# RWKV heads: nine wide elementwise products per head pair move from VectorE to GpSimd, and three preparation steps change places

## The reference

```python
r, k, v, wl, al, gl = jnp.split(pm, [...], axis=-1)
w = -jax.nn.softplus(-(decay_w0 + jnp.tanh(wl) @ decay_w2)) - 0.5      # decay, as a log rate
a = jax.nn.sigmoid(iclr_a0 + al @ iclr_a2)                             # rate
g = jax.nn.sigmoid(gl) @ gate_g2                                       # gate
kk = k * k_k
kk = kk / jnp.maximum(jnp.sqrt(jnp.sum(kk * kk, axis=-1)), 1e-12)      # unit keys
k = k * (1.0 + (a - 1.0) * k_a)                                        # k_mod
decay = jnp.exp(-jnp.exp(w))
def step(S, inp):
    sa = jnp.einsum('bhvk,bhk->bhv', S, kk_t)
    S = S * d_t - sa[..., None] * (kk_t * a_t) + v_t[..., None] * k_t
    return S, jnp.einsum('bhvk,bhk->bhv', S, r_t)
S, y = lax.scan(step, s0, ...)
yn = (y - mean(y)) * rsqrt(var(y) + GN_EPS) * lnx_w + lnx_b            # per head
bonus = sum(r * k * r_k) * v
return (yn + bonus) * g
```

## Time and profile before

| | us |
|---|---|
| median of 3 runs | 3746.51 |
| lowest and highest | 3738.27, 3763.45 |
| the profiled execution's own time | 3749.47 |
| its span, first to last instruction | 3747.8 |
| PE busy | 3337.5 (89%) |
| DVE busy | 3037.3 (81%) |
| ACT busy | 1127.8 (30%) |
| POOL busy | 1597.2 (43%) |
| mean granted TensorE clock | 0.936 of full speed |

### The profile page before, as it was taken

How to read it: one execution, slowest core, us unless ns; L and a number is a source line. 1 busy time by engine, 2 the same in 40 slices (tenths; PEclk the granted TensorE clock), 3 DMA queues, 4 the chain that set the end, 5 groups by cost and what they waited for, 6 DMA issues and landing times.

```text
span 3747.8 us, 62513 instructions
## 1 busy us (share of the span) xinstructions
PE 3337.5 (89%) x21071; PEld 3085.6 (82%) x21071; DVE 3037.3 (81%) x6175; ACT 1127.8 (30%) x2153; POOL 1597.2 (43%) x1407
## 2 busy tenths in 40 slices
PE   7998848888887998847779999999999999999997
PEld 7998736666676755547779999999999999999997
DVE  6543656676664689989789999999999999999997
ACT  3101433233231222369722222222222222222221
POOL 1120001111110133520067776767777676676772
PEclk9999778787898999979989999999999999999998
DMA  3222330010004001024699999999999999999995
GB/s 122 97 87 78 111 103 7 22 33 13 1 10 160 13 26 37 15 93 190 247 348 362 356 352 339 353 348 366 353 348 359 350 355 349 334 363 347 350 356 188
DMA packets 296942, 781.44 MB, mean 209 GB/s; under 512 B 28376, under 2 KB 129240, under 8 KB 295424
## 3 DMA queue, kind: packets, MB, share of 16 engines
q0 software_dynamic: 135568, 493.54, 35.9%
q1 hardware_dynamic: 161264, 286.56, 21.4%
HBM read 709.32 MB, written 70.11 MB: 208 GB/s over the span
## 4 chain that ended last, share of the span: by engine, by line
PE 30%; DVE 9%; issue 7%; DMA 6%; POOL 2%; DVEq 1%; ACT 1%; POOLq 0%; ACTq 0%; SPq 0%
PE experts_down_ps L113 7%; PE experts_down_ps L114 7%; PE experts_down_ps L115 7%; DMA stream_u<-in_up_rows,experts_u_at 4%; PE experts_up_ps L114 3%; PE experts_up_ps L113 3%; PE experts_up_ps L115 3%; DVE stream_u L3315 2%; DVE stream_h_rows_of L3332 2%; DMA stream_u<-in_down,experts_v_at 2%; POOL stream_u L3102 1%; DVE stream_h L3338 1%; DVE picking_mean_square L2880 1%; DVE stream_h_rest L2880 1%; POOL stream_u L3087 1%
## 5 line engine op out<-in xcount | busy, mean ns | idle before, releaser
L3087 POOL DMA_INDIRECT stream_u<-in_up_rows,experts_u_at x448 | 600.2, 1340 | 316.6 <-DVE experts_dot L3315 150.1
L3102 POOL DMA_INDIRECT stream_u<-in_down,experts_v_at x448 | 588.6, 1314 | 253.3 <-issue 95.7
L113 PE MATMUL experts_up_ps<-experts_u_hi,experts_up_hi 128*128 128x320 f32 x2048 | 634.8, 310 | 33.5 <-DVE experts_up_lo L3286 27.2
L113 PE MATMUL experts_down_ps<-experts_act_hi,experts_down_hi 128*128 128x320 f32 x2048 | 640.6, 313 | 21.0 <-DVE stream_h L3338 15.7
L114 PE MATMUL experts_down_ps<-experts_act_lo,experts_down_hi 128*128 128x320 f32 x2048 | 636.1, 311 | 0.0
L115 PE MATMUL experts_down_ps<-experts_act_hi,experts_down_lo 128*128 128x320 f32 x2048 | 636.1, 311 | 0.0
L114 PE MATMUL experts_up_ps<-experts_u_lo,experts_up_hi 128*128 128x320 f32 x2048 | 634.1, 310 | 0.0
L115 PE MATMUL experts_up_ps<-experts_u_hi,experts_up_lo 128*128 128x320 f32 x2048 | 634.0, 310 | 0.0
L3332 DVE SCALAR_TENSOR_TENSOR stream_h_rows_of<-stream_u,experts_weight,stream_h_rows_of 128x1024 f32<-128x1024 f32 x448 | 568.1, 1280 | 30.4 <-DMA stream_u<-in_down,experts_v_at 19.0
L3315 DVE CUSTOM_DVE_ANT_0 stream_u<-stream_u,stream_u_rows_of 128x1024 f32<-128x1024 f32 x448 | 544.7, 1216 | 40.3 <-DMA stream_u<-in_up_rows,experts_u_at 40.2
L113 PEld LDWEIGHTS experts_up_ps<-experts_u_hi,experts_up_hi 128*128 128x128 f32 x2048 | 385.7, 188 | 34.7 <-DVE experts_up_lo L3286 34.2
(11 more groups left out here) (463 smaller groups left out, 6143.7 us busy)
## 6 DMA issues: line engine op xcount, KB each, us to landing
stream_h_rest<-in_up SPq DMA_DIRECT2D x128, 512.0 KB, 7.1
stream_u<-in_down_pieces SPq DMA_DIRECT2D x128, 512.0 KB, 6.3
gates<-spread_spread SPq DMA_DIRECT2D x10, 4096.0 KB, 11.5
experts_gates<-gates SPq DMA_DIRECT2D x64, 640.0 KB, 9.9
cols<-inp_done POOLq DMA_DIRECT2D x26, 576.0 KB, 3.8
inp_w_in<-in_w_in SPq DMA_DIRECT2D x27, 512.0 KB, 4.4
pick_w_query<-in_w_query SPq DMA_DIRECT2D x14, 512.0 KB, 4.0
stream_u<-in_up_rows,experts_u_at POOLq DMA_INDIRECT x448, 7.1
```

The costliest lines, as they stand in the source:

```text
L113: pe.matmul(out, w_hi, x_hi, start=start, stop=False)
L3087: pool.indirect_dma_start((half_row if i == HALF_DOT else u_row[b]), None, up_rows_d, bass.IndirectOffsetOnAxis(ap=u_at[slot][:, col:col + ...
L3102: pool.indirect_dma_start((half_row if i == HALF_ADD else v_row[b]), None, v_table, bass.IndirectOffsetOnAxis(ap=v_at[slot][:, col:col + 1 ...
```

## The change

For pairs 1 to 3, five products of the preparation (`in_log`, `before_log`, `k_mod`, `kk`, `b`) are issued on GpSimd, in two functions: `logs` in g2 of the pair before, and `unit_keys` in g3, each ahead of that group's `list_blocks`. For pairs 0 to 2, the four products of the epilogue go to GpSimd as `normed_y`, in g1 after the stores of the sample states. New semaphores `prep_pool` and `ep_pool` count them. The first pair's preparation and the last pair's epilogue stay on VectorE. Besides, `norm` moves from steps 9 to 11 to steps 6 to 8 and `gate` from 6 to 8 to 9 to 11; the exponentials move from steps 6 to 9 to steps 9 to 12, the clipping from 12 to 9, the reciprocals of the norm from 13 to 15 to 10 to 12, and `weighted` from 17 to 16.

```diff
@@ -1003,12 +1003,13 @@
-PREP_PE = ("decay0", "decay1", "decay2", "rate0", "rate1", "rate2", "gate0", "gate1", "gate2", "norm0", "norm1", "norm2",
+PREP_PE = ("decay0", "decay1", "decay2", "rate0", "rate1", "rate2", "norm0", "norm1", "norm2", "gate0", "gate1", "gate2",
            "bonus0", "bonus1", "bonus2")
-PREP_ACT = ("decay0", "decay1", "square", "decay2", "rate0", "rate1", "rate2", "gate0", "exp_inv", "gate1", "exp_in", "gate2",
-            "exp_before", "exp_next", "exp_seq", "norm0", "norm1", "norm2")
-PREP_DVE = ("kk_raw", "less_ka", "log_rate", "cum", "mid", "in_log", "before_log", "next_diff", "next_log", "k_scale", "k_mod",
-            "clipped", "inverse0", "inverse1", "inverse2", "kk", "b", "weighted", "bonus0", "bonus1", "bonus2")
+PREP_ACT = ("decay0", "decay1", "square", "decay2", "rate0", "rate1", "rate2", "norm0", "norm1", "norm2", "gate0", "exp_inv", "gate1", "exp_in", "gate2",
+            "exp_before", "exp_next", "exp_seq")
+PREP_DVE = ("kk_raw", "less_ka", "log_rate", "cum", "mid", "next_diff", "next_log", "k_scale",
+            "clipped", "inverse0", "inverse1", "inverse2", "weighted", "bonus0", "bonus1", "bonus2")
+PREP_POOL = ("in_log", "before_log", "k_mod", "kk", "b")
...
-DECAY_AT, RATE_AT, GATE_AT, NORM_AT, INVERSE_AT, BONUS_AT = 0, 3, 6, 9, 13, 19
+DECAY_AT, RATE_AT, NORM_AT, GATE_AT, EXP_AT, INVERSE_AT = 0, 3, 6, 9, 9, 10
...
-EP_VEC = ("mean0", "mean1", "var0", "var1", "mean2", "var2", "inverse0", "inverse1", "inverse2", "scaled", "affine", "with_bonus", "gated")
+EP_VEC = ("mean0", "mean1", "var0", "var1", "mean2", "var2", "inverse0", "inverse1", "inverse2")
+EP_POOL = ("scaled", "affine", "with_bonus", "gated")
...
+def on_pool(j, name):
+    return j > 0 and name in PREP_POOL
...
+        def wait_prepared(eng, j, name):
+            if on_pool(j, name):
+                eng.wait_ge(prep_pool, reached(PREP_POOL, j, name))
+            else:
+                eng.wait_ge(prep_vec, reached(PREP_DVE, j, name))
+
+        def mid_log_args(pre):
+            by_tile = [buf[:].rearrange("p (c t) -> p c t", c=NT) for buf in (pre.in_decay, cum)]
+            return *by_tile, mid[:, 0:NT].unsqueeze(2).broadcast_to([P, NT, P])
...
+                def made(j, name):
+                    pool.wait_ge(ep_pool, reached(EP_POOL, j, name))
+
+                def normed_y(j):
+                    y, pre = y_of[j % 2], prepared[j % 2]
+                    pool.wait_ge(ep_vec, reached(EP_VEC, j, "inverse2"))
+                    pool.tensor_tensor(y[:], y[:], pre.inv_decay[:], ALU.mult).then_inc(ep_pool, 1)
+                    made(j, "scaled")
+                    pool.tensor_scalar(y[:], y[:], coef(j, C_LNW), coef(j, C_LNB), ALU.mult, ALU.add).then_inc(ep_pool, 1)
+                    made(j, "affine")
+                    pool.wait_ge(prep_vec, reached(PREP_DVE, j, "bonus2"))
+                    pool.tensor_tensor(y[:], y[:], pre.bonus[:], ALU.add).then_inc(ep_pool, 1)
+                    made(j, "with_bonus")
+                    pool.tensor_tensor(y[:], y[:], pre.gate[:], ALU.mult).then_inc(ep_pool, 1)
+
+                def logs(j, pre):
+                    out, sums, mids = mid_log_args(pre)
+                    pool.wait_ge(prep_vec, reached(PREP_DVE, j, "mid"))
+                    pool.tensor_tensor(out, sums, mids, ALU.subtract).then_inc(prep_pool, 1)
+                    wait_prepared(pool, j, "in_log")
+                    pool.tensor_tensor(pre.before_decay[:], pre.in_decay[:], pre.before_decay[:], ALU.subtract).then_inc(prep_pool, 1)
+                    pool.wait_ge(prep_vec, reached(PREP_DVE, j, "k_scale"))
+                    pool.tensor_tensor(pre.k_mod[:], pre.k_mod[:], k[:], ALU.mult).then_inc(prep_pool, 1)
+
+                def unit_keys(j, pre):
+                    pool.wait_ge(prep_vec, reached(PREP_DVE, j, "inverse2"))
+                    pool.tensor_tensor(pre.kk[:], pre.kk[:], tmp[:], ALU.mult).then_inc(prep_pool, 1)
+                    wait_prepared(pool, j, "kk")
+                    pool.tensor_tensor(pre.b[:], pre.kk[:], pre.b[:], ALU.mult).then_inc(prep_pool, 1)
...
-                    pool.wait_ge(ep_vec, reached(EP_VEC, j, "gated"))
+                    if j < PAIRS - 1:
+                        made(j, "gated")
+                    else:
+                        pool.wait_ge(ep_vec, reached(EP_VEC, j, "gated"))
...
+                    following = group.j + 1 < PAIRS
+                    if group.g == 2 and following:
+                        logs(group.j + 1, prepared[1 - group.x])
+                    if group.g == 3 and following:
+                        unit_keys(group.j + 1, prepared[1 - group.x])
...
+                            normed_y(group.j - 1)
                             store_y(group.j - 1, P)
...
-                    if step == 6:
-                        act.wait_ge(prep_vec, reached(PREP_DVE, j, "in_log"))
+                    if step == EXP_AT:
+                        wait_prepared(act, j, "in_log")
                         act.activation(pre.inv_decay[:], pre.in_decay[:], ACT.Exp, scale=-1.0).then_inc(prep_act, 1)
...
+                    if step == EXP_AT + 1:
+
+                        wait_prepared(act, j, "before_log")
...
-                    if step == 8:
...
-                    if step == 9:
...
-                    if step == 6 and j >= 2:
-
-                        act.wait_ge(ep_vec, reached(EP_VEC, j - 2, "gated"))
+                    if NORM_AT <= step < NORM_AT + 3:
+                        third(j, "norm", step - NORM_AT, tmp, ACT.Sqrt)
+                    if step == GATE_AT and j >= 2:
+
+                        act.wait_ge(ep_pool, reached(EP_POOL, j - 2, "gated"))
                     if GATE_AT <= step < GATE_AT + 3:
                         third(j, "gate", step - GATE_AT, pre.gate, ACT.Copy)
                     exponents(step, j, pre)
-                    if NORM_AT <= step < NORM_AT + 3:
-                        third(j, "norm", step - NORM_AT, tmp, ACT.Sqrt)
...
                         own(j, "mid")
-                        dve.tensor_tensor(pre.in_decay[:].rearrange("p (c t) -> p c t", c=NT), by_tile,
-                                          mid[:, 0:NT].unsqueeze(2).broadcast_to([P, NT, P]), ALU.subtract).then_inc(prep_vec, 1)
+                        if j == 0:
+                            out, sums, mids = mid_log_args(pre)
+                            dve.tensor_tensor(out, sums, mids, ALU.subtract).then_inc(prep_vec, 1)
                     if step == 6:
-                        own(j, "in_log")
-                        dve.tensor_tensor(pre.before_decay[:], pre.in_decay[:], pre.before_decay[:], ALU.subtract).then_inc(prep_vec, 1)
+                        if j == 0:
+                            own(j, "in_log")
+                            dve.tensor_tensor(pre.before_decay[:], pre.in_decay[:], pre.before_decay[:], ALU.subtract).then_inc(prep_vec, 1)
...
-                    if step == 8:
+                    if step == 8 and j == 0:
                         own(j, "k_scale")
                         dve.tensor_tensor(pre.k_mod[:], pre.k_mod[:], k[:], ALU.mult).then_inc(prep_vec, 1)
-                    if step == 12:
+                    if step == NORM_AT + 3:
                         from_act(j, "norm2")
                         dve.tensor_scalar(tmp[:], tmp[:], 1e-12, None, ALU.max).then_inc(prep_vec, 1)
                     if INVERSE_AT <= step < INVERSE_AT + 3:
                         own(j, "clipped")
                         inverse_norm(step - INVERSE_AT)
                     if step == 16:
-                        own(j, "inverse2")
-                        dve.tensor_tensor(pre.kk[:], pre.kk[:], tmp[:], ALU.mult).then_inc(prep_vec, 1)
-                    if step == 17:
                         own(j, "kk")
-                        dve.tensor_tensor(pre.b[:], pre.kk[:], pre.b[:], ALU.mult).then_inc(prep_vec, 1)
-                    if step == 17:
                         weigh(j, pre, tmp)
+                    if step == BONUS_STEPS[0] and j >= 2:
+                        dve.wait_ge(ep_pool, reached(EP_POOL, j - 2, "gated"))
...
-                        from_act(group.j, "exp_before" if group.j == 0 else "norm2")
+                        from_act(group.j, "exp_before")
...
-                        if point == 4:
-                            scaled(group.j - 1)
-                            affine(group.j - 1)
-                        if point == 5:
-                            gated(group.j - 1)
```

More of the change, by code:

```diff
@@ L1018 @@
                "gate0", "gate1", "gate2", "norm1", "norm2"),
+    PREP_POOL: (),
     PREP_DVE: ("kk_raw", "less_ka", "log_rate", "cum", "mid", "in_log", "before_log", "next_diff", "next_log", "k_scale", "k_mod",
@@ L1235, in _ @@
                 for j in range(PAIRS - 1):
-                    sp.wait_ge(prep_vec, reached(PREP_DVE, j, "k_mod"))
+                    wait_prepared(sp, j, "k_mod")
                     sp.wait_ge(qk_ready, j * GROUP_COUNT)
@@ L1353, in prepare_first @@
```

(4 more changed lines are left out.)

8 lines of the change are left out of this document (4 added, 4 removed).

## The result

| | before | changed |
|---|---|---|
| median, us | 3746.78 | 3763.57 |
| lowest and highest, us (20 runs each) | 3734.86, 3766.25 | 3754.03, 3778.96 |
| ratio, 95% interval | | 1.0047 [1.0034, 1.0061] |
| profiled execution, own time and span, us | 3749.47, 3747.8 | 3763.18, 3761.5 |

The account below looks back on a forecast made before the run. No engine is full; ordered hand-offs bound the RWKV stage, VectorE across g1 and g2. Terms of 3.8 + 1.9 + 1.0 - 2.9 = 3.8 us a pair, 11.4 for three, gave 3758 us, range 3722 to 3786.

Parts of the forecast that it names:

- Prices on GpSimd: Moved products on GpSimd: 2.62 us each, `affine` 1.8; 68 us in all beside 93.5 busy of 620.
- The library reload: GpSimd, ahead of the first `affine`: comes once, taken as 0 on the path, at most 4 us.
- The stalls: VectorE held by GpSimd's products: `normed_y` in g1 +3.8 us a pair, `logs` in g2 +1.9.
- All pairs alike: RWKV stage: 3.8 us a pair, taken for three pairs as 11.4 us.
- ScalarE, -2.9 a pair: ScalarE in the RWKV stage: 1.16 + 1.78 us a pair given back, from the exponential and the norm.
- The early reciprocals, +2: Norm's three reciprocals, three slots earlier in late g2: cost between 0 and 5.1 us, taken as 2.
- `kk` and `b` gone from C, -2.7: VectorE behind the solve in g3: `kk` and `b` are gone, 2.7 us saved a pair.
- My bound on what a clock gives back: TensorE after the VectorE-bound stretch: of 7 us at half clock at most 3.5 us would come back.
- Rival B: RWKV stage: stalls don't reach the path; 11.3 us a pair shed, 3713 us, or 3729 with half; chance 0.27.
- Rival C: GpSimd's queue becomes late in g2 and g3, TensorE's spread and the solve wait: 3789 us; chance 0.12.
- the 1.6 us forecast for a late solve: g3: `unit_keys` ahead of GpSimd's list makes the solve about 1.6 us late; bounds in time or 4 us.
- Rival D: Nothing is moved on the path; other waits, TensorE's state chain, end last: 3746 us; chance 0.13.

Follow-up runs that it names:

- run 3: Changed kernel with the epilogue's four products back on VectorE; new order kept, the preparation's five products on GpSimd: 3749.32 us, ratio 0.9999 to the kernel before.
- run 4: Changed kernel, but with pair 2's epilogue, which runs beside pair 3, back on VectorE: 3748.85 us, ratio 1.0000 to the kernel before.
- run 6: New order with all nine products on VectorE, but clip and norm reciprocals back at steps 12 to 15: 3744.61 us, ratio 0.9980 to the kernel before.
- run 1: Changed kernel with all nine products a pair back on VectorE, leaving the new order alone: 3772.29 us, ratio 1.0065 to the kernel before.

## Why the prediction was right, and where it wasn't

The total and the class came out; the sum's terms did not all do so.

- **Prices on GpSimd.** A product that nothing holds up 2.61 us (2.62 forecast), `affine` 1.30 (1.8), `in_log`, with one small broadcast input, 2.35; `kk` and `k_mod`, which met VectorE's work, 2.93 and 3.00 in pair 1. The idle engine's room was as computed. The library reload cost nothing to see: `affine` began 0.11 us behind `scaled`.
- **The stalls.** Right in kind and nearly in size. `normed_y`: 2.41 + 0.96 + 2.29 + 2.27 = 7.9 us against 5.0 removed, so +2.9 (3.8 forecast, `affine` being most of the difference). `logs`: 1.92 + 2.42 against 2.71, so +1.6 (1.9). Changed kernel against run 3, A of pair 1: 40.0 - 36.8 = 3.2.
- **All pairs alike: wrong.** I multiplied by three. In pair 3 the same stalls meet a stretch that ran short (23.9 us), and cost 8.7 with the clock's fall, taken back with run 4. It was there to be seen: the stretch of the earlier trace rows had lost its clock already, that of pair 3 hadn't.
- **ScalarE, -2.9 a pair: right in sign, its size open.** A of pairs 0 to 2 is 3.1, 5.1 and 4.6 us shorter in run 6 than before, and the wait for `in_log` is gone; by the medians run 6 is 7.5 us below, 2.5 a pair. The table load ahead of the norm isn't gone, it stands earlier (at 768.65): 13 loads as before, and the three new ones of 1.28 that the forecast names.
- **The early reciprocals, +2: the step that failed.** I took their direct time, between 0 and 5.1 us, and nothing for the clock. Run 1 against run 6 has B at 32.4 against 20.0: +12.4 (+9.5 and +11.6 in pairs 0 and 2). The row that I should have weighed was TensorE's clock in that stretch, 1.00 with VectorE busy 18.8 of 19.8 us: a place with no air, and with a clock to lose.
- **`kk` and `b` gone from C, -2.7: mis-sized too**, the other way: C is 9.9 us shorter (run 3 against run 1), as a fallen clock came back. `weighted`, a step earlier, has an unknown part in that. My bound on what a clock gives back was made for a stretch of 7 us, not for 20.
- The two errors are of one kind and nearly cancel: from before to changed, C is 11.0, 16.8 and 10.7 us shorter in pairs 0 to 2, B 14.1, 14.6 and 14.6 longer. (C of before is itself 37.7 us in pair 1 and 31.6 to 31.9 in pairs 0 and 2, so pair 1 alone flatters C.) That the total came out is in part luck. For run 1, which has the early reciprocals without the products, the same terms give +2 - 2.9, about 1 us a pair below before; measured is 22 us above (24 by the ratio), some 8 a pair.
- **Rival B** (the stalls don't reach the path) fell: A, where the stalls are, is 40.0 us in pair 1 of the changed kernel, not 37.9, though six operations (7.7 us) left VectorE there. **Rival C** (GpSimd's queue late) wasn't seen: TensorE's waits for the solution's spread on GpSimd are 5.2 us in the stage, 6.9 before. The list in g3 does start later (after `unit_keys`, which end at 815.4), but nobody stands long for it: TensorE has no wait on GpSimd in B or C of pair 1, so the 1.6 us forecast for a late solve don't show. **Rival D** has a part of the truth: run 3 moves five products a pair and ends within 0.1% of the kernel before.
